# Banks of two feed-forward blocks, and the order of two steps in cross attention, in a hybrid decoder layer

## The reference

```python
def cross_attend(h, mk, mv, lp):
    B, T, _ = h.shape
    q = rms_norm((h @ lp['w_xq']).reshape(B, T, X_HEADS, X_DIM), lp['g_xq'])
    s = jnp.einsum('bthd,bnhd->bhtn', q, mk).astype(jnp.float32) * (X_DIM ** -0.5)
    p = jax.nn.softmax(s, axis=-1).astype(mv.dtype)
    o = jnp.einsum('bhtn,bnhd->bthd', p, mv).reshape(B, T, X_HEADS * X_DIM)
    return o @ lp['w_xo']

def ffn(h, lp):
    u = jnp.maximum(h @ lp['w_ff1'], 0)
    return (u * u) @ lp['w_ff2']

    # in the layer
    x = x + cross_attend(rms_norm(x, lp['g_x']), mk, mv, lp)
    x = x + ffn(rms_norm(x, lp['g_ff']), lp)
```

## Time and profile before

| | us |
|---|---|
| median of 3 runs | 1145.97 |
| lowest, highest | 1140.49, 1147.19 |
| the profiled execution, its own time | 1146.07 |
| its span | 1143.9 |
| PE busy in the span | 1110.4 (97%) |
| DVE, ACT, POOL busy | 735.6, 488.9, 394.6 |

### The profile page before, as it was taken

How to read it: one execution, slowest core, us unless ns; L and a number is a source line. 1 busy time by engine, 2 the same in 40 slices (tenths; PEclk the granted TensorE clock), 3 DMA queues, 4 the chain that set the end, 5 groups by cost and what they waited for, 6 DMA issues and landing times.

```text
span 1143.9 us, 22255 instructions
## 1 busy us (share of the span) xinstructions
PE 1110.4 (97%) x8120; PEld 1006.3 (88%) x8120; DVE 735.6 (64%) x1294; ACT 488.9 (43%) x1066; POOL 394.6 (34%) x236
## 2 busy tenths in 40 slices
PE   7999999999999999999999998899999999999998
PEld 4799797567899999999969984899999999999997
DVE  1649653687566677666757547888667558647742
ACT  5231114455554455545522245556137326515711
POOL 0117124450176767767631210331132215203200
PEclk9999999999999999999999998999999999999999
DMA  9422102032354445344306232213212312321202
GB/s 361 164 93 93 60 1 65 1 106 99 100 157 119 127 121 154 109 137 118 99 1 237 77 111 93 93 56 130 82 49 83 140 37 80 125 91 63 86 1 83
DMA packets 62276, 114.43 MB, mean 100 GB/s; under 512 B 6658, under 2 KB 41635, under 8 KB 62115
## 3 DMA queue, kind: packets, MB, share of 16 engines
q1 hardware_dynamic: 61602, 111.33, 29.8%
q0 software_dynamic: 576, 1.84, 0.5%
HBM read 107.90 MB, written 5.25 MB: 99 GB/s over the span
## 4 chain that ended last, share of the span: by engine, by line
PE 83%; DVE 7%; ACT 3%; issue 3%; POOL 2%; DMA 1%; POOLq 0%; SPq 0%; DVEq 0%; ACTq 0%
PE bank L1557 17%; PE bank L1517 8%; PE bank L913 6%; PE bank L1263 6%; PE bank L1265 5%; PE bank L1332 5%; PE bank L1264 5%; PE bank L931 3%; PE bank L1219 3%; PE bank L875 2%; PE bank L1505 2%; POOL stat L3152 2%; PE bank L1093 2%; PE bank L1173 2%; PE bank L1487 1%
## 5 line engine op out<-in xcount | busy, mean ns | idle before, releaser
L1557 PE MATMUL bank<-ur,wr 128*128 128x288 f32 x1488 | 199.5, 296 | 0.0
L1557 PEld LDWEIGHTS bank<-ur,wr 128*128 128x128 f32 x1488 | 198.6, 189 | 0.0
L3152 POOL TENSOR_TENSOR stat<-stat,cst 128x32 f32<-128x32 f32 x32 | 175.2, 5476 | 2.5
L1517 PE MATMUL bank<-hr,wr 128*128 128x288 f32 x1176 | 158.6, 295 | 0.9 <-ACT hT L2125 0.9
L1517 PEld LDWEIGHTS bank<-hr,wr 128*128 128x128 f32 x1176 | 157.2, 188 | 1.7 <-ACT hT L2125 1.6
L1263 PE MATMUL bank<-wq_high,c_parts 128*128 128x288 f32 x512 | 157.3, 307 | 1.0 <-ACT mixT L1902 1.0
L1265 PE MATMUL bank<-wq_low,c_parts 128*128 128x288 f32 x512 | 152.4, 298 | 0.0
L1264 PE MATMUL bank<-wq_high,c_parts 128*128 128x288 f32 x512 | 151.1, 295 | 0.0
L2556 DVE TENSOR_REDUCE stat<-hT 128x8 f32<-128x512 f32 x128 | 86.7, 682 | 66.1 <-ACT hT L1920 64.2
L2076 ACT CAST wr<-ring 128x512 fp32r<-128x512 f32 x114 | 67.2, 619 | 113.9 <-PE bank L1557 105.8
L3183 POOL TENSOR_TENSOR hT<-ring 128x512 f32<-128x512 f32 x28 | 40.4, 1442 | 217.5 <-DVE wr L2730 161.5
(11 more groups left out here) (452 smaller groups left out, 2240.9 us busy)
## 6 DMA issues: line engine op xcount, KB each, us to landing
ring<-in_ring_w_dram SPq DMA_DIRECT2D x106, 512.0 KB, 4.0
arena<-in_page_rows_dram SPq DMA_DIRECT2D x128, 144.0 KB, 2.2
hT<-in_ckv_t_dram SPq DMA_DIRECT2D x64, 128.0 KB, 2.0
arena<-in_ckv_t_dram SPq DMA_DIRECT2D x64, 128.0 KB, 2.1
arena<-in_mk_t_dram SPq DMA_DIRECT2D x8, 512.0 KB, 4.9
arena<-in_cache_mv_dram SPq DMA_DIRECT2D x8, 512.0 KB, 7.0
mixT<-in_x_dram SPq DMA_DIRECT2D x1, 2048.0 KB, 12.5
out_dram<-hf SPq DMA_DIRECT2D x8, 256.0 KB, 2.0
```

The lines of the kernel that those rows point to most:

```text
L1517: ins = mm(o[:, 0:HALF], wr[:, m % OPERANDS, ew, k * P:(k + 1) * P], hr[:, X_OF[name], ex, k, :], start=(start and k == 0 and n == 0), sto ...
L1557: ins = mm(bank[PLAN["f2", q, j, c][0]][:, 0:HALF], wr[:, m % OPERANDS, ew, k % HK * P:(k % HK + 1) * P], ur[:, eu, k, c * HALF:(c + 1) * ...
L3152: G.tensor_tensor(r, r, power.broadcast_to([P, 32]), ALU.pow).then_inc(S("r_pg"), 1)
```

## The change

Three edits. The plain blocks' results move: block 0 from banks 0 and 1 to banks 1 and 2, block 1 from banks 2 and 3 to banks 0 and 3; blocks 2 and 3 stay. On PE, the scores of the last two sample sequences come ahead of the turning of prompt pair 7. On DVE, the division of prompt pair 6 comes ahead of `values_low(1)` and `sample_max(1)`. No instruction is added or removed.

```diff
@@ make_plan
     for j in range(PLAIN):
         for c in range(2):
-            fill(("plain", j, c), 2 * j + c)
+            fill(("plain", j, c), ((1, 2), (0, 3), (4, 5), (6, 7))[j][c])
@@ PE
             sample_scores(4)
             sample_scores(5)
             turned_prompt(6)
-            turned_prompt(7)
             sample_scores(6)
             sample_scores(7)
+            turned_prompt(7)
             turned_sample(0)
             turned_sample(1)
             prompt_values(2)
@@ DVE
             prompt_max(6)
             prompt_max(7)
             sample_shares(0)
+            prompt_shares(6)
             values_low(1)
             sample_max(1)
-            prompt_shares(6)
             prompt_shares(7)
             sample_shares(1)
             sample_max(2)
```

## The result

| | before | after |
|---|---|---|
| median of 19 runs, us | 1145.97 (1140.01 to 1148.56) | 1148.55 (1144.36 to 1151.66) |
| ratio, 95% interval | | 1.0025 (1.0014 to 1.0037) |
| the profiled execution, its own time and span | 1146.07, 1143.9 | 1149.73, 1147.6 |

What follows compares the result with a forecast made beforehand. PE, busy 1110.4 of 1143.9 us, was taken as the bound, so only its idle or slow time could be won. From 1146.07, -1.8 (banks), +1.2 (clock) and +1.2 (cross attention) gave +0.6, 1146.7 us; range 1141.0 to 1148.8.

Steps and rivals of the forecast that it cites:

- What moves where: Plain blocks and cross attention: plain(0) unheld, plain(2) waits 2.9 us for part 7, last sample scores some 2.4 for bank 0.
- the prediction's 757.0: Plain blocks: the time in us at which plain(2) was reckoned to begin before the change, against 755.2 after it.
- The banks' gain of 1.8 us: Plain blocks: plain(2) begins at 755.2 instead of 757.0, and what follows keeps the gain, -1.8 us.
- the 1.2 us for the new fall: Behind the new gap ahead of plain(2): the clock likely falls, costing 0 to 1.7 us, taken as +1.2.
- Cross attention, +1.2: Cross attention: waiting for bank 0 delays turned pair 7 and sample_exponentials(3), +0.24 to +1.5 us, taken as +1.2.
- the lower end, 0.24: Cross attention: the smallest price of the two orders, sample_exponentials(3) ending at 703.5, with PE at 2.4 GHz.
- before's 703.0: Cross attention on ACT: the time in us at which sample_exponentials(3) ended before, from which its delay was counted.
- The sum: Whole kernel: -1.8 for banks, +1.2 for the new gap's clock, +1.2 for cross attention, +0.6 us net, 1146.7.
- Bank 0 and the clock decide: Rival, last sample scores and new gap: both costs in full, 1.5 + 1.7 - 1.8 = +1.4 us, 1147.5; chance 0.18.
- The order gains as meant: Rival, cross attention: sample scores not held by bank 0, no cost there, net -0.6 us, 1145.5; chance 0.10.
- Both clocks kind: Rival: no fall behind the new gap, PE at 2.4 GHz in the sample scores, -1.6 us, 1144.5; chance 0.17.
- The whole wait comes back: Rival, plain blocks: plain(2) isn't held, wait and slow stretch both regained, -4.7 us, 1141.4; chance 0.05.

Runs made afterwards that it cites:

- e2: Only PE's order changed (last sample scores ahead of turned pair 7), old banks, against the kernel before: ratio 1.0007 (0.9991 to 1.0023).
- e16: The changed kernel timed a third time, against the kernel before: ratio 1.0031 (1.0015 to 1.0046).
- e1: Only the plain blocks' banks moved, old orders, against the kernel before: ratio 1.0000 (0.9986 to 1.0015).
- e5: The changed kernel timed a second time, against the kernel before: ratio 1.0020 (1.0004 to 1.0037).
- e4: PE's and DVE's new orders together with the old banks, against the kernel before: ratio 1.0014 (0.9997 to 1.0032).
- e8: Both orders, old banks, PE making pair 6's transposes five times over, against the kernel before: ratio 1.0002 (0.9982 to 1.0022).
- e12: New banks, old orders, POOL's weight sums behind weight part 9's low part, 16 constant products ahead of turned pair 6, against before: ratio 0.9966 (0.9950 to 0.9982).
- e13: Both orders, old plain banks, sample pair 3's scores in bank 3 instead of 0, against the kernel before: ratio 1.0032 (1.0014 to 1.0050).
- e17: Both orders, old plain banks, sample pair 3's scores in bank 4 instead of 0, against the kernel before: ratio 0.9997 (0.9976 to 1.0017).
- e11: New banks, old orders, POOL's weight sums starting only behind the low part of weight part 9, against before: ratio 0.9957 (0.9940 to 0.9974).
- e15: The kernel before timed against itself: ratio 1.0014 (0.9997 to 1.0031).
- e9: The kernel before with 20 products of constants filling PE's wait ahead of plain(0), against before: ratio 1.0002 (0.9985 to 1.0019).
- e10: New banks, old orders, 20 products of constants filling PE's wait ahead of plain(2), against before: ratio 0.9995 (0.9978 to 1.0011).

## Why the prediction was wrong, point by point

- **What moves where.** Right. `plain(0)` starts without a wait, `plain(2)` waits for weight part 7, counted 2.9 and measured 3.1. The last sample scores wait for bank 0, counted 2.4 and measured 2.42. ACT's copy of pair 7 holds the sample exponentials, and the low part of part 7 is made 1.0 us later than before, counted 1.2. In the trace `plain(2)` began 67.66 us behind the scores, 0.65 sooner than the 68.3 that the prediction's 757.0 makes; banks and cross attention together had been put at 0.6.
- **The banks' gain of 1.8 us and the 1.2 us for the new fall.** This is the step that failed: the sum -1.8 + 1.2 for banks and clock together. The 757.0 in it held 1.68 us of fallen clock behind the old gap; take that out and the gain is 0.2 (755.4 against 755.2). That fall was credited in full, while the new one was entered with 1.2 of its 1.7. Measured from the first matmul of the output projection, `plain(2)` began at 43.33 us in before, at 41.79 in after, and at 41.80 in e2, which has the old banks and no fall. So the "gain" of 1.5 between before and after is the old fall, and nothing else. The new fall then cost 1.5 (14.51 us for blocks 2 and 3, against e16's 12.98), and the whole stretch was 56.13 against 56.07. The two gaps are of one length and their falls of one price, so the two terms should have made 0, with a spread to both sides. Over all traces the plain stretch is 55.97 for the eight with old banks, unfilled, and 55.68 for the four with the new (after, e1, e5, e16), with single values from 54.59 to 57.17. So the -0.6 was credit for luck.
- **Cross attention, +1.2.** The mechanism was right. The size came near (+0.96 between the traces of before and after), but its parts were mixed. Seven traces with the old orders and nothing filled there have 24.34 to 24.91, mean 24.70; four with both orders (after, e4, e5, e16) 25.87, 26.50, 26.45, 25.41, mean 26.06: +1.36. But the lower end, 0.24, was counted against before's 703.0, which holds a fallen clock too: the same one-sided entry. At a kept clock on both sides (e8, e12) the orders cost 0.93, and only about 0.4 of the 1.36 is the slower clock. So the wait for bank 0, with ACT's copy behind it, is most of the price: with the bank out of the way the last share stands at 14.04 (e13, e17), with it and a busy PE at 14.80 (e8).
- **The sum.** With the steps mended it is 0 + 1.4, or 1.1 by the means of the two stretches, not +0.6. The three timings say +2.9, +2.3 and +3.5. Over all runs on record (43 of after, 194 of before) the means are 1148.2 and 1146.2, which is +2.0 (about 1.3 to 2.7). The granted clock averages 0.9910 over 163 runs of before and 0.9898 over 43 of after, which is 0.0012 x 1147 x 2 = 2.7 us more at the 1.2 GHz level. That loses at most 1.4 us, less where PE was idle, and part of it is the slow clock already in the traces' 1.1. So some 0.9 us of the 2.0 (or 1.8 of the first ratio's 2.9) isn't located: the stretches ahead of the change hold identical work, and the kernel before against itself differed by 1.6. It stays open whether it is anything but the error of such timings.
- **The rivals.** "Bank 0 and the clock decide" (+1.4), given 0.18, comes nearest to the average and is e5's trace (+1.5). "The order gains as meant" fell, even with a free bank. "Both clocks kind" is nearest to e16's trace: scores to end 454.2, 1.0 below before's (counted 1.6), with the clock kept behind the new gap and through the last sample scores, though not behind them (cross 25.41). "The whole wait comes back" was given 0.05, since nothing in the change brings DVE forward; e11 shows that with the new banks POOL's sums were all that stood in its way.

## What to carry to other kernels

Before a wait is priced, split off the clock that fell behind it, and enter that on both sides of the sum or on neither: a wait that only moves takes its fall along. Follow a freed engine to its next wait, and name the next user of each bank or buffer that an order touches; here the gaps only changed their place, and one of my own repairs made the same mistake. A filler that outlasts the wait measures itself, so it can't compare two gaps. What paid was making the late engine early: one wait on POOL, on top of banks that were worth nothing alone, gave back 4.9 us.

## What the runs showed of the hardware

The granted clock behind an idle stretch of PE of 3.0 to 3.1 us, with the same work ahead of it, went down to the 1.2 GHz level (27.28 us for 192 matmuls, before and e15), for longer (28.40, e8), or not at all (25.81, e2; 12.98 for 96, e16). The prediction had taken a fall behind the new gap as likely, and had entered the old one as certain. Where a wait was filled by matmuls (e8, e9, e10, e12), the clock stood at 1.00 behind that wait every time. The prediction's sentence that by "TensorE: Matmul & The Clock Gate" of the Trainium skill it is partly luck which gap is followed by a fall agrees with these traces, and it should have changed the sum on both sides.
